# Moving the token gather of the next expert turn and splitting the scatter in a mixture-of-experts loop

## What is computed

```python
def moe_swiglu(h, router_w, router_b, w_gate, w_up, w_down):
    t = h.reshape(B * S, D)                              # 256 x 1024
    logits = (t @ router_w) + router_b
    top_vals, top_idx = lax.top_k(logits, TOP_K)         # 2 of 8 experts
    top_w = jax.nn.softmax(top_vals, axis=-1)
    combine = sum(one_hot(top_idx) * top_w[..., None])   # 256 x 8
    out = 0
    for e in range(N_EXPERTS):
        y = (silu(t @ w_gate[e]) * (t @ w_up[e])) @ w_down[e]   # 1024 -> 3584 -> 1024
        out = out + combine[:, e:e + 1] * y
    return out
```

## Time and profile before

| | value |
|---|---|
| median of 3 executions | 2921.37 us |
| the profiled execution | 2915.98 us, its span 2913.8 us |
| TensorE busy (matmul) | 2792.6 us, 96% of the span |
| VectorE busy | 1992.6 us, 68% |
| ScalarE busy | 1681.5 us, 58% |
| mean granted TensorE clock | 0.986 |
| read from HBM | 690.99 MB |
| expert turns in the trace | 9, the first gather at 817.47 us, the last scatter at 1981.61 us |

### The profile page before, as it was taken

How to read it: one execution, slowest core, us unless ns; L and a number is a source line. 1 busy time by engine, 2 the same in 40 slices (tenths; PEclk the granted TensorE clock), 3 DMA queues, 4 the chain that set the end, 5 groups by cost and what they waited for, 6 DMA issues and landing times. The chain is left out here.

```text
span 2913.8 us, 38993 instructions
## 1 busy us (share of the span) xinstructions
PE 2792.6 (96%) x15406; PEld 2325.2 (80%) x15407; DVE 1992.6 (68%) x2084; ACT 1681.5 (58%) x1961; POOL 20.1 (1%) x45
## 2 busy tenths in 40 slices
PE   7999999999989999999999999998999999999999
PEld 4779899788978778787877878787867898857897
DVE  4656555576587979888887988885565555474555
ACT  3574444567366777777676777675344445343544
POOL 0000000000000000000000000001000000000000
PEclk9999999999989999999999999999999999999999
DMA  9747443856489989898989989975413453414451
GB/s 342 270 165 253 174 176 124 292 174 205 166 293 364 326 325 365 325 365 326 363 327 347 342 322 366 325 258 180 159 64 138 171 201 129 173 58 145 160 194 73
DMA packets 311121, 693.84 MB, mean 238 GB/s; under 512 B 7254, under 2 KB 26180, under 8 KB 310996
## 3 DMA queue, kind: packets, MB, share of 16 engines
q1 hardware_dynamic: 309040, 689.07, 65.8%
q0 software_dynamic: 1344, 2.82, 0.4%
q10 hardware_dynamic: 612, 0.18, 0.0%
HBM read 690.99 MB, written 1.05 MB: 238 GB/s over the span
## 5 line engine op out<-in xcount | busy, mean ns | idle before, releaser
L2518 DVE TENSOR_TENSOR ring_rest<-ring,weights_hi 128x2048 fp32r<-128x2048 f32 x270 | 605.1, 2284 | 34.9 <-ACT weights_hi L1894 33.9
L1894 ACT ACTIVATE weights_hi<-ring 128x2048 fp32r<-128x2048 f32 x270 | 514.3, 1920 | 127.4 <-PE ps L1661 80.7
L1659 PE MATMUL ps<-weights_hi,xg_hi 128*128 128x512 f32 x1008 | 405.3, 402 | 3.5 <-DVE xg_lo L2518 3.5
L1661 PE MATMUL ps<-weights_hi,xg_lo 128*128 128x512 f32 x1008 | 397.5, 394 | 0.0
L1660 PE MATMUL ps<-ring_rest,xg_hi 128*128 128x512 f32 x792 | 312.6, 395 | 0.0
L1894 ACT ACTIVATE arena<-ps 128x512 f32<-128x512 f32 (+6 forms) x307 | 157.2, 529 | 228.4 <-PE ps L1661 51.9
L1678 PE MATMUL ps<-weights_hi,hidden_split_moe 128*128 128x512 f32 x1008 | 284.2, 393 | 0.0
L2518 DVE TENSOR_TENSOR ring_rest<-ring,mix_hi 128x2048 fp32r<-128x2048 f32 (+2 forms) x76 | 171.1, 2254 | 137.4 <-ACT mix_hi L1894 137.1
L2518 DVE TENSOR_TENSOR w_split<-ring,w_split 128x1024 fp32r<-128x1024 f32 x128 | 150.8, 1222 | 164.7 <-ACT w_split L1894 164.7
L1894 ACT ACTIVATE arena<-arena 128x256 f32<-128x256 f32 (+5 forms) x309 | 152.4, 518 | 175.1 <-DVE arena L2518 74.5
L2518 DVE TENSOR_TENSOR late_rest<-arena,weights_hi 128x2048 fp32r<-128x2048 f32 x108 | 244.6, 2285 | 6.6 <-ACT weights_hi L1894 4.5
(11 more groups left out here) (295 smaller groups left out, 5330.8 us busy)
## 6 DMA issues: line engine op xcount, KB each, us to landing
ring<-in_moe_w_gate_dram SPq DMA_DIRECT2D x54, 2048.0 KB, 7.7
ring<-in_moe_w_up_dram SPq DMA_DIRECT2D x45, 2048.0 KB, 7.8
ring<-in_moe_w_down_dram SPq DMA_DIRECT2D x36, 2048.0 KB, 7.7
ring<-in_mlp_w_dram SPq DMA_DIRECT2D x32, 2048.0 KB, 8.7
arena<-in_moe_w_down_dram SPq DMA_DIRECT2D x27, 2048.0 KB, 7.8
ring<-in_w_mod_dram SPq DMA_DIRECT2D x48, 1024.0 KB, 9.2
ring<-in_w_in_dram SPq DMA_DIRECT2D x48, 1024.0 KB, 5.9
arena<-in_moe_w_up_dram SPq DMA_DIRECT2D x18, 2048.0 KB, 7.8
```

Source lines behind the costliest of these rows:

```text
L1659: pe.matmul(b, xg_hi[:, k, :], hi[:, i, :], start=(k == 0), stop=False)
L1661: mm = pe.matmul(b, xg_lo[:, k, :], hi[:, i, :], start=False, stop=(k == KD - 1))
L1894: return act.activation(o, i, func, **kw)
L2518: return dve.tensor_tensor(o, a, b, op)
```

## The change

- The scatter of the turn before no longer stands at the start of the turn. It is two pairs of tiles: columns 0 to 511 behind the second piece of up 0, columns 512 to 1023 behind the second piece of up 1 (event "scatter").
- Each scatter tile is two one-pass products instead of one fp32 product: the 0/1 matrix `to_tokens_hot` (fp32r) times the rounded part `y_hi` and times the rest `y_lo`. The router weight goes into `gated_y`: `slot_weight` is the sum of each slot's row of `to_tokens`, which ScalarE accumulates with the copy, and the two products become `scalar_tensor_tensor`.
- New on ScalarE: `round_y`, twice a turn. New on VectorE: `rest_of_y`, twice a turn, and `tokens_hot`, once a turn.
- The gather for turn e+1 is issued in turn e behind the second piece of up 6 (event "gather"), ahead of the two pieces of down 5 and the two of down 6. Its modulation, rounding and rest follow there (`round_tokens`, `rest_of_tokens`), the rest and the rounding in two halves. The gather for turn 0 stands ahead of the loop (`first_gather`), and the last turn gathers for a turn that doesn't follow.
- At the start of a turn ScalarE rounds pieces 0 to 4, then `y_hi`, then piece 5. VectorE takes rests 0 to 2, then `gated_y`, rest 3, `rest_of_y(0)`, rest 4.
- GpSimd's load of `gain_row` also waits for the last tokens' split. Some buffers lie in other places.

The core of the diff:

```diff
@@ expert_events
+        if what == "up" and half and g < 2:
+            events.append(("scatter", g))
+        if (what, g, half) == ("up", GROUPS - 1, 1):
+            events.append(("gather",))
@@ gpsimd
             pool.wait_ge(pe_done, value["moe_down", TURNS - 1, GROUPS - 1])
+            pool.wait_ge(sem("xg_split_ready"), 2 + 2 * TURNS)
@@ tensor
-            def scatter(open_tile, last_y):
...
-                        done(pe.matmul(b, to_tokens[:, t * P:(t + 1) * P], y_slots[:, c * 512:(c + 1) * 512],
-                                       start=True, stop=True))
+            def scatter(b, t, c, y_part):
+                hot = to_tokens_hot[:, t * P:(t + 1) * P]
+                pe.matmul(b, hot, y_part, start=True, stop=False)
+                done(pe.matmul(b, hot, y_lo[:, c], start=False, stop=True))
...
                     pe.wait_ge(sem("moe_rest_ready"), (p + 1) + e * n_pieces)
+                    if p < 2:
+                        pe.wait_ge(sem("xg_split_ready"), (p + 1) + e * 2)
...
+                    if g == 0 and half == 0:
+                        pe.wait_ge(acc_emptied, base_acc + 1 + e)
...
+                    elif kind == "scatter":
+                        c = at[0]
+                        if c == 0:
+                            pe.wait_ge(sem("to_tokens_hot_ready"), 1 + e)
+                        pe.wait_ge(sem("y_split_ready"), (c + 1) + e * 2)
+                        for t in range(TT):
+                            scatter(open_at(lambda i: ("scatter", i, c, t), e), t, c, y_hi[:, :])
+                    elif kind == "gather":
+                        pe.wait_ge(sem("to_slots_ready"), 2 + e)
+                        gather(lambda half: open_at(lambda i: ("gather", i, half), e))
@@ scalar
+            def round_y(c, dst, e):
+                act.wait_ge(sem("y_gated"), (c + 1) + e * 2)
+                f(dst, y_slots[:, c * 512:(c + 1) * 512], ACT.Copy).then_inc(sem("y_rounded"), 1)
+            def round_tokens(b, gathered, evicted, second_evicted):
+                act.wait_ge(pe_done, gathered)
+                for k in range(4):
+                    ins = f(xg[:, k], b[:, k * P:(k + 1) * P], ACT.Identity,
+                            scale=scale[:, k:k + 1], bias=shift[:, k:k + 1])
+                ins.then_inc(emptied["act"], 1)
+                for half in range(2):
...
+                    f(xg_hi[:, 4 * half:4 * half + 4, :], xg[:, 4 * half:4 * half + 4], ACT.Copy)\
+                        .then_inc(sem("xg_rounded"), 1)
...
-                for p in range(4):
+                for p in range(5):
                     round_piece(p)
...
-                for p in range(4, HI_BUFFERS):
-                    round_piece(p)
+                round_y(0, y_hi[:, :], e)
+                round_piece(5)
...
+                    elif kind == "scatter":
+                        if at[0] == 0:
+                            act.wait_ge(pe_done, step_at(lambda i: ("scatter", i, 0, TT - 1), e))
+                            round_y(1, y_hi[:, :], e)
...
-                        f(to_tokens, acc(1, 0)[:, 0:T], ACT.Copy).then_inc(sem("to_tokens_ready"), 1)
+                        f(to_tokens, acc(1, 0)[:, 0:T], ACT.Copy, accum_out=slot_weight)\
+                            .then_inc(sem("to_tokens_ready"), 1)
@@ vector
-                    ins = tt(y_slots[:, c * 512:(c + 1) * 512], acc(0, c), gb[:, 1, c * 512:(c + 1) * 512], ALU.mult)
-                ins.then_inc(acc_emptied, 1)
+                    stt(y_slots[:, c * 512:(c + 1) * 512], acc(0, c), slot_weight,
+                        gb[:, 1, c * 512:(c + 1) * 512], ALU.mult, ALU.mult).then_inc(sem("y_gated"), 1)
+            def rest_of_y(c, rounded_part, e):
+                dve.wait_ge(sem("y_rounded"), (c + 1) + e * 2)
+                tt(y_lo[:, c], y_slots[:, c * 512:(c + 1) * 512], rounded_part.bitcast(F32), ALU.subtract)\
+                    .then_inc(sem("y_split_ready"), 1)
...
-                rest_of_piece(0)
-                rest_of_piece(1)
+                for p in range(3):
+                    rest_of_piece(p)
                 gated_y(piece_done(-1, e))
...
-                add_scattered(0)
-                add_scattered(1)
...
-                add_scattered(2)
-                add_scattered(3)
-                for p in range(2, HI_BUFFERS - 1):
-                    rest_of_piece(p)
+                rest_of_piece(3)
+                rest_of_y(0, y_hi[:, :], e)
+                dve.sem_inc(acc_emptied, 1)
+                rest_of_piece(4)
...
+                        if (what, g, half) == ("gate", 1, 0):
+                            rest_of_y(1, y_hi[:, :], e)
+                    elif kind == "scatter":
+                        add_scattered(at[0])
+                    elif kind == "gather":
+                        rest_of_tokens(bank(("gather", 0, 1)), step_at(lambda i: ("gather", i, 1), e), e + 1)
...
+                    else:
+                        tokens_hot(e + 1)
```

More of the change, by code:

```diff
@@ L352, in experts @@
     def experts(self):
+        self.add(("first_gather", 0), "act")
+        self.add(("first_gather", 1), "dve")
         for e in range(TURNS):
[L354 to L357, removed]
             for kind, *at in expert_events():
@@ L661, in program @@
         xn_moe = expert.cut(TT, D)
-        to_slots = expert.cut(TT, P)
-        weighted = expert.cut(TT, P)
+        to_slots = Region(rope1_at, TT * P).cut(TT, P)
+        to_tokens_at = expert.pos
         to_tokens = expert.cut(T)
@@ L667, in program @@
         y_slots = expert.cut(D)
+        weighted = Region(y_at, TT * P).cut(TT, P)
+        y_hi_at = expert.pos
+        expert.cut(512)
         route_at = expert.pos
@@ L1708, in skipped @@
                 pe.sem_inc(pe_done, turn_steps)
+            pe.wait_ge(sem("to_slots_ready"), 1)
+            gather(lambda half: open_bank(("first_gather", half)))
             for j in range(4):
-                wait_emptied(pe, plan.rotation[plan.bank["gather", 0, 0] - 1 - j])
+                wait_emptied(pe, plan.rotation[plan.bank["first_gather", 0] + 1 - j])
             over_turns(pe, expert_turn, skipped)
-            freed_seen["dve"] = plan.nth["scatter", TURNS - 1, 2 * TT - 1]
-            freed_seen["act"] = plan.nth["moe_gate", TURNS - 1, GROUPS - 1]
-            scatter(lambda i: open_bank(("last_scatter", i)), lambda: wait_y(TURNS))
+            freed_seen["dve"] = plan.nth["moe_up", TURNS - 1, 0]
+            freed_seen["act"] = plan.nth["moe_gate", TURNS - 1, 0]
+            pe.wait_ge(sem("to_tokens_hot_ready"), 1 + TURNS)
+            for i in range(2 * TT):
+                if i < 2:
+                    pe.wait_ge(sem("y_split_ready"), 2 * TURNS + i + 1)
+                scatter(open_bank(("last_scatter", i)), i // 2, i % 2, last_y_hi[:, i % 2])
+            pe.wait_ge(acc_emptied, base_acc + 1 + TURNS)
             acc_uses[0] += TURNS + 1
@@ L2342, in skipped @@
                 act.sem_inc(sem("to_tokens_ready"), 1)
+                act.wait_ge(sem("y_rounded"), e * 2)
+                act.sem_inc(sem("y_rounded"), 2)
+            taken[0] += 1
+            round_tokens(bank(("first_gather", 0)), value["first_gather", 0], plan.nth["first_gather", 0],
+                         plan.nth["first_gather", 1])
             over_turns(act, expert_turn, skipped)
             taken[0] += TURNS * turn_empties["act"]
+            for c in range(2):
+                round_y(c, last_y_hi[:, c], TURNS)
             f(st[:, 2 * TT + 2:2 * TT + 3], eps, ACT.Sqrt)
@@ L3051, in _ @@
             find_slots(0)
+            tokens_hot(0)
             scale, shift = modc[:, 1, 3 * KD:4 * KD], modc[:, 1, 2 * KD:3 * KD]
@@ L3058, in gated_y, with rest_of_tokens, rest @@
                 for c in range(2):
-                    ins = tt(y_slots[:, c * 512:(c + 1) * 512], acc(0, c), gb[:, 1, c * 512:(c + 1) * 512], ALU.mult)
-                ins.then_inc(acc_emptied, 1)
+                    stt(y_slots[:, c * 512:(c + 1) * 512], acc(0, c), slot_weight,
[4 more added lines that the diff above has]
+                    .then_inc(sem("y_split_ready"), 1)
+            def rest_of_tokens(b, gathered, e):
+                def rest(half):
+                    dve.wait_ge(sem("xg_rounded"), (half + 1) + e * 2)
+                    tt(xg_lo[:, 4 * half:4 * half + 4, :], xg[:, 4 * half:4 * half + 4],
+                       xg_hi[:, 4 * half:4 * half + 4, :].bitcast(F32), ALU.subtract).then_inc(sem("xg_split_ready"), 1)
+                dve.wait_ge(pe_done, gathered)
+                for i in range(4):
+                    k = 4 + i
+                    ins = ts(xg[:, k], b[:, i * P:(i + 1) * P], scale[:, k:k + 1], ALU.mult,
+                             shift[:, k:k + 1], ALU.add)
+                ins.then_inc(emptied["dve"], 1)
+                rest(0)
+                rest(1)
             def expert_turn(e):
@@ L3130, in _ @@
             gated_y(value["moe_down", TURNS - 1, GROUPS - 1])
+            for c in range(2):
```

(2 more changed lines are left out.)

77 lines of the change are left out of this document (41 added, 36 removed).

## The result

The changed kernel takes 2932.68 us (median of 6 executions, 2928.41 to 2938.19), the kernel before, measured beside it, 2919.47 us (6 executions, 2915.72 to 2924.41). The ratio is 1.0043, 95% interval 1.0029 to 1.0057: slower by 12.6 us, 8.5 to 16.6. The predicted time was 2939, its range 2921 to 2950, and slower was the likeliest sign.

The account below looks back on a forecast made before the run. The prediction took TensorE to set the pace of the expert turns. It added 5.6 us for eight turn distances, 8.0 for the last turn and 4.0 for the first, +17.6, to the median 2921.4: 2939, range 2921 to 2950.

Parts of the forecast that it names:

- Part 1: Gather moved ahead of down 5: still 3.74 us of TensorE a turn, and what follows it costs nothing.
- Part 2: Scatter as eight one-pass matmuls: 1.86 us a turn in place of 3.69.
- The rival in which the product with `y_hi` runs at the fp32 rate: Scatter: 3.7 us a turn instead of 1.86, the wait shrinking as much, 2939 again; 3%.
- Part 3: Turn start: TensorE waits 0.98 us each turn for piece 0's chain, with the table load staying at the loop's head.
- Part 4: Behind the turn start: TensorE waits 2.2 us for VectorE's queue up to the first hidden rest, mostly ahead of down 0.
- The turn: Sum of a turn's terms with three slow first matmuls: 129.4 us against 128.7 before, +5.6 us over eight distances.
- The third rival: Clock falls in the new waits, half clock for 4 us each: 1.7 us a turn, about +16, 2955; 8%.
- Part 5: Last turn: +8.0 us from an unused gather, the previous turn's scatter and waiting; the shorter scatter behind it saves 0.
- Part 6: First turn: first tokens ahead of piece 0 in both queues, first gate piece at 831.8 instead of 827.83, +4.0 us.
- The sum: Whole kernel: 5.6 + 8.0 + 4.0 = +17.6 us, a median of 2939.
- The fast rival: Turn start closes, all waits of Part 3 and Part 4 absent: a turn of 125.9 us, 2909 in all; 13%.
- The rival that let the head load go: Table load at the loop's head goes, piece 0 rounded 1.4 us sooner: a turn of 127.9, 2925 in all; 12%.

Follow-up runs that it names:

- e5: Changed kernel with the edits of e1 and e2 together; 2902.29 us, ratio 0.9943 to the kernel before.
- e8: e5 with the scatter as one fp32 product, without rounding and rest of the gated sums; ratio 1.0005 to the kernel before.
- e7: Changed kernel with two one-column activations of other tables ahead of each turn's first weight rounding, one more table load; ratio 1.0097 to the kernel before.
- e2: Changed kernel with VectorE taking a turn's first hidden rest ahead of weight rest 10; ratio 0.9995 to the kernel before.
- e1: Changed kernel with the last hidden group's second half rounded and split into its own buffer, one down piece sooner; ratio 0.9986 to the kernel before.
- e6: e5 with VectorE alone modulating, rounding and splitting the first turn's tokens; 2900.24 us, ratio 0.9936.
- e9: e5 with the two one-column activations of e7; ratio 0.9981 to the kernel before.

## Why the prediction was right, step by step

**Part 1, the gather moved: right.** It is 3.73 us at its new place and nothing waits for what follows it; e5 with no wait in any turn shows it best.

**Part 2, the scatter: right in the price of the new form, a little off in that of the old one.** The split pairs (two tiles) take 0.93 each, 1.86 in all. The 3.69 of the old one runs to the end of its last matmul, while 1.86 counts from start to start. By e5 and e8 the saving is 1.6, not 1.83. It does not touch the sum, which was built from the new work. The rival in which the product with `y_hi` runs at the fp32 rate is out: the scatter's matmuls start 0.23 us apart.

**Part 3, the turn start: right.** Predicted a wait of 0.98; A is 0.88 longer than undisturbed (27.61 against 26.73). The profile's own 0.72 is smaller, since the matmul behind the wait lasts 0.50 instead of 0.39. The load stands where I left it, and e7 shows that one load more costs little over its length. One reading was off without touching the sum: of the 6.9 us of waits ahead of scatters, 3.35 is that of the closing scatter behind the last turn, not of a turn.

**Part 4, VectorE's queue: right.** Predicted 2.2; B is 2.35 longer than undisturbed. The hidden rest was to begin at 25.9 and began at 26.1. Some 0.5 of the 2.35 lies in small stops ahead of the last scatter matmul (forecast 0.4), the rest ahead of down 0 and in its restart. That VectorE's queue is the cause is shown twice: an earlier place in it (e2) and an earlier start of it (e1) each take most of the delay away. The two `scalar_tensor_tensor` are 1.40 together, which is in the bound that I gave.

**The turn: 129.4 predicted, 128.96 measured.** The delay of 3.2 was right; two small terms were not. I added 0.3 for three slow first matmuls. Of these only the one behind the wait for down 0 comes on top (down 0 starts 2.23 late, the gate piece behind it 2.35); the other two fall into the wait that follows them, so they stood in the sum twice. And the undisturbed turn is 125.74, not 120.34 + 3.74 + 1.86 = 125.94, because the gather's 3.74 too runs to the end of its last matmul. The distance in the trace of before is 128.7, so a plain turn cost 0.24 and not 0.7.

**The third rival came in part.** Of the eight distances, six are 128.6 to 129.0 and two are 130.51 and 130.53. In these the granted clock fell behind the wait ahead of down 0. The window, and TensorE's matmuls at half rate (columns x2 and x4: 0.63 and 1.09 us in a plain turn):

```profile
1374.00:1383.00 9.00, 7.44 (x26) 5.34 (x25) 9.00 (x7) 3.99 (x3) 0.00 (x0) 0.84 0.98 357
```

```profile
1379.43 0.73 PE L1692 MATMUL ps<-weights_hi,hidden_split_moe 128*128 128x512 f32 x2 [1.53 <-DVE hidden_split_moe L2575]
1380.00 1.01 PE L1692 MATMUL ps<-ring_rest,hidden_split_moe 128*128 128x512 f32 x2
1380.80 1.91 PE L1692 MATMUL ps<-weights_hi,hidden_split_moe 128*128 128x512 f32 x4
```

Each fall costs 1.55 us; I had 1.7 from the earlier trace rows and had given the rival all eight turns or none. It came in two. So the eight distances' +4.7 are 8 x 0.24 = 1.9 of waits and some 2.8 of clock, where I had forecast 5.6 of waits. Their sum came near for a reason that was only half mine; the other half was luck.

**Part 5, the last turn: right.** Predicted +8.0, measured +7.7. The tail behind was to save nothing: from the last down matmuls to the next stage's first it was 1993.68 - 1977.64 = 16.04, and is 2015.01 - 1998.78 = 16.23.

**Part 6, the first turn: the chain right, its size a quarter too large in this execution.** Predicted +4.0 (its terms add up to 831.7, so 3.9), measured +3.0 from gather to gate. The gather took 5.63 in place of 6.37 in this execution, and the chain behind VectorE's half 6.35 in place of 6.54. The first gather's length differs from execution to execution: it takes 5.67 to 6.62 in e1 to e6, and from gather to gate it is 13.41 to 14.37 in e1 to e5, so +3.0 to +4.0. TensorE then started at half clock, after 7.75 us of idle time:

```profile
836.68 0.79 PE L1671 MATMUL ps<-weights_hi,xg_hi 128*128 128x512 f32 x1 [7.75 <-DVE ring_rest L2575]
...
863.54 0.73 PE L1692 MATMUL ps<-weights_hi,hidden_split_moe 128*128 128x512 f32 x2 [0.15 <-DVE hidden_split_moe L2575]
```

```profile
836.00:840.00 4.00, 3.32 (x8) 2.65 (x9) 4.00 (x3) 4.00 (x4) 0.00 (x0) 0.50 0.00 0
```

It cost nothing here: down 0 starts 26.86 us behind the gate piece, as in every turn, and the wait ahead of it is 0.15 instead of 1.54. I had said that part of it would fall into that wait; all of it did. Where that wait is gone it does cost: in e5 the first distance is 127.92 where the others are 125.74, and the window at its head shows why.

```profile
830.68:836.00 5.32, 5.32 (x14) 4.21 (x15) 5.32 (x4) 5.10 (x4) 0.00 (x0) 0.55 0.00 2
```

**The sum.** Touched parts +15.4 in the profiled pair against 17.6 forecast, 12.6 (8.5 to 16.6) in the medians. The fast rival (no waits, 125.9 a turn, 2909) was a true picture of a kernel that wasn't this one: e5 is it, with 125.74 and 2902. It took one change at the head of ScalarE's chain and one swap in VectorE's queue, at the two points that the rival was to be decided on. The rival that let the head load go, 12%, stays out: the load is there in every turn.

## What to carry to other kernels

Before moving work off the start of a loop's turn, ask which chains it was covering: here a gather and a scatter gave VectorE 8 us to get ahead, and without them TensorE met the end of a chain (rounding, table load, rounding, rest) and then a queue. Replay the queues of the stretch behind the moved work, instruction by instruction; average spare time (19 us a turn on VectorE) did not show it. And when a saving on one engine is paid for on another, measure it from start to start, and expect its sign to follow the engine that is late in that stretch: the split scatter was worth -0.6 us a turn in one order of the queues and +1.6 in another.

## What the hardware showed that I had not expected

The same wait of 1.53 to 1.54 us brought a fall of the granted clock in two of eight turns and none in the other six, with the same instructions in all eight; I found nothing in the traces that tells beforehand where it falls. What a fall costs depends on what stands behind it. Behind the wait ahead of down 0 it costs 1.55 us. In e7 the clock fell behind the longer wait at the turn start in five of eight turns (0.72 over 1227 to 1233 us) and not in the other three (1.00 over 966 to 972), and the distances are 130.50 all the same, because the VectorE queue sets down 0 in either case: the wait there was 0.51 where it had fallen and 1.54 where it had not.

```profile
966.00:972.00 6.00, 5.94 (x26) 4.82 (x27) 6.00 (x5) 5.79 (x5) 0.00 (x0) 1.00 0.85 319
...
1227.00:1233.00 6.00, 5.94 (x19) 4.74 (x20) 6.00 (x5) 5.77 (x5) 0.00 (x0) 0.72 0.85 319
```

```profile
992.93 0.73 PE L1692 MATMUL ps<-weights_hi,hidden_split_moe 128*128 128x512 f32 x2 [1.54 <-DVE hidden_split_moe L2577]
...
1253.92 0.73 PE L1692 MATMUL ps<-weights_hi,hidden_split_moe 128*128 128x512 f32 x2 [0.51 <-DVE hidden_split_moe L2577]
```

In the traces of e1, e2, e5, e8 and e9, where the wait ahead of down 0 is 0.30 us or none, no turn but the first is longer for this reason.

A trace is one execution, and the granted clock differs from one execution to the next of the same kernel, with the time: e5 took 2896.59 us at 0.987 and 2908.47 at 0.980. In e8 three executions took 2914.2 to 2914.9 at 0.984 and six took 2922.8 to 2928.0 at 0.977 to 0.981. So a few us of a whole kernel are read from ratios of many executions, and the distances of turns from traces.
